# Hybrid decoder step on one core: the down-projections' high and low activation parts side by side, three matmuls under the high weights instead of four

## The reference, cut to what matters

```python
def conv_ffn(h, buf, w_up, conv_w, conv_b, w_down):
    up = h @ w_up
    padded = concatenate([buf, up], axis=1)
    c = conv_b
    for j in range(3):
        c = c + conv_w[j] * padded[:, j:j + l]
    g, v = split(c, 2, axis=-1)
    return (silu(g) * v) @ w_down, padded[:, -2:]
...
x = x + conv_ffn(rmsnorm(x, norm_ffn[i]), ...)
```

## Time and profile before

| | |
|---|---|
| median of 3 runs | 1355.78 us (1355.6, 1355.78, 1358.63) |
| span of the profiled execution, first to last instruction | 1349.1 us |
| the profiled execution's own time | not listed apart from its span |
| TensorE busy | 1239.3 us, 92%, 9702 matmuls |
| weight loads | 1168.9 us, 87%, beside the matmuls |
| VectorE busy | 723.9 us, 54% |
| ScalarE busy | 450.3 us, 33% |
| GpSimd busy | 371.5 us, 28% |
| DMA | 129.12 MB, mean 96 GB/s |

### The profile page before, as it was taken

One profiled execution on the slowest core, in us unless ns is written; L12 is line 12 of the kernel. 1 busy time (PEld: TensorE's weight loads), 2 busy tenths in 40 slices (PEclk: granted clock), 3 DMA queues, 4 the chain that ended last, 5 costly groups with the idle time before them and its releaser, 6 DMA issues.

```text
span 1349.1 us, 25331 instructions
## 1 busy us (share of the span) xinstructions
PE 1239.3 (92%) x9702; PEld 1168.9 (87%) x9710; DVE 723.9 (54%) x1164; ACT 450.3 (33%) x748; POOL 371.5 (28%) x802
## 2 busy tenths in 40 slices
PE   5249869989999999999999799999999999999999
PEld 4249446679999999999998766699999999999998
DVE  5036316756777833777633645045577752477732
ACT  5012224433544412444443112133354431344420
POOL 1003576777777777500002145000000000000000
PEclk9669758999999999999997579599999999999999
DMA  6132121013233432222655313022222232222232
GB/s 203 36 129 83 54 67 40 24 48 116 95 117 109 136 114 99 97 93 93 230 142 138 95 55 108 14 86 88 92 89 87 89 108 95 79 93 93 93 105 97
DMA packets 52918, 129.12 MB, mean 96 GB/s; under 512 B 18124, under 2 KB 21964, under 8 KB 52832
## 3 DMA queue, kind: packets, MB, share of 16 engines
q1 hardware_dynamic: 49920, 117.93, 26.5%
q0 software_dynamic: 2944, 10.49, 2.0%
HBM read 109.89 MB, written 18.21 MB: 95 GB/s over the span
## 4 chain that ended last, share of the span: by engine, by line
PE 82%; DMA 5%; DVE 5%; SPq 4%; ACT 3%; issue 1%; ACTq 0%; DVEq 0%
PE ps L1278 23%; PE ps L1280 23%; PE ps L1279 23%; DMA kc<-in_cache_k 4%; PE ps L1521 4%; SPq L270 3%; PE ps L1517 2%; PE ps L1473 2%; ACT probs L679 2%; DMA w_raw<-in_wqkv 1%; PE ps L1478 1%; DVE probs L1038 1%; PE ps L1369 1%; DVE soft L1022 1%; PE ps L1438 1%
## 5 line engine op out<-in xcount | busy, mean ns | idle before, releaser
L1278 PE MATMUL ps<-hx_hi,w_hi 128*128 128x260 f32 x1600 | 454.1, 284 | 45.4 <-DVE w_lo L829 42.8
L1280 PE MATMUL ps<-hx_hi,w_lo 128*128 128x260 f32 x1600 | 453.2, 283 | 0.0
L1279 PE MATMUL ps<-hx_lo,w_hi 128*128 128x260 f32 x1600 | 451.7, 282 | 0.0
L578 ACT ACTIVATE w_hi<-w_raw 128x1024 fp32r<-128x1024 f32 (+1 forms) x156 | 175.8, 1127 | 548.2 <-PE ps L1280 498.8
L1278 PEld LDWEIGHTS ps<-hx_hi,w_hi 128*128 128x128 f32 x1600 | 302.4, 189 | 46.6 <-issue 43.0
L1279 PEld LDWEIGHTS ps<-hx_lo,w_hi 128*128 128x128 f32 x1600 | 302.2, 189 | 0.1
L1280 PEld LDWEIGHTS ps<-hx_hi,w_lo 128*128 128x128 f32 x1600 | 302.1, 189 | 0.0
L829 DVE TENSOR_TENSOR w_lo<-w_raw,w_hi 128x1024 fp32r<-128x1024 f32 (+1 forms) x156 | 207.7, 1332 | 150.2 <-ACT w_hi L578 150.2
L1278 PE MATMUL ps<-hid_hi,w_hi 128*128 128x260 f32 x704 | 199.1, 283 | 0.0
L1279 PE MATMUL ps<-hid_lo,w_hi 128*128 128x260 f32 x704 | 198.8, 282 | 0.0
L1280 PE MATMUL ps<-hid_hi,w_lo 128*128 128x260 f32 x704 | 198.6, 282 | 0.0
(11 more groups left out here) (224 smaller groups left out, 1776.5 us busy)
## 6 DMA issues: line engine op xcount, KB each, us to landing
w_raw<-in_wup SPq DMA_DIRECT2D x88, 512.0 KB, 3.2
w_raw<-in_wdn SPq DMA_DIRECT2D x32, 704.0 KB, 4.0
w_raw<-in_wglu SPq DMA_DIRECT2D x16, 512.0 KB, 3.2
w_raw<-in_wqkv SPq DMA_DIRECT2D x12, 512.0 KB, 4.4
w_raw<-in_wo SPq DMA_DIRECT2D x8, 512.0 KB, 3.3
g_scr<-rec POOLq DMA_DIRECT2D x8, 512.0 KB, 3.0
c_scr<-rec POOLq DMA_DIRECT2D x8, 512.0 KB, 3.1
wst<-g_scr SPq DMA_DIRECT2D x8, 512.0 KB, 8.1
```

Source lines behind the costliest of these rows:

```text
L578: act.activation(w_hi[b][:, 0:kt * P], w_raw[b][:, 0:kt * P], ACT.Copy).then_inc(hi_done, 1)
L1278: pe.matmul(out, wh, xh, start=(k == 0), stop=False)
L1279: pe.matmul(out, wh, xl, start=False, stop=False)
L1280: ins = pe.matmul(out, wl, xh, start=False, stop=(k == kt - 1))
```

## The change: what it does

The hidden tiles' high and low parts, so far in two arrays, lie in one array `hid_x` with a row of `WX` = 1040 columns for each of the 11 tiles: the high part of the first half (260 columns) followed by 86 columns of its low part, the same for the second half, and then the other 174 low columns of both halves (348 together). `down_unit` replaces `unit` in the four down stages. For each input tile it streams 346, 346 and 348 columns through the high weights and, as before, 260 and 260 through the low weights. High products and the low weights' products accumulate in columns 0 to 260 of the unit's two banks; the low parts' products land in columns 260 to 346 of those banks and in a third bank, 4 + b.

A unit's result is thus in two parts. ScalarE copies the low parts' products to a buffer in SBUF with two activations (172 and 348 columns), after its split of the next weights; VectorE waits for the first copy, adds the main part to `x`, waits for the second copy, adds the buffer to `x`, and then counts `evac`. `hid_hi` is written to two pieces of a row by one instruction, `hid_lo` by two instructions. In dn01 the buffer is `lo_rec`, which lies over `rec`, and ScalarE waits for `scr_out` ahead of the stage; in the other down stages it is `lo_part`. `rec` grows by 16 columns, and its uses name their columns; those lines of the diff are left out below.

```diff
--- before.py
+++ after.py
@@ -31,6 +31,10 @@
+LA = 86
+LC = HALF - LA
+WA, WC = HALF + LA, 2 * LC
+WX = 2 * WA + WC
@@ -96,8 +100,7 @@
-        hid_hi, D0 = place("hid_hi", NPAIR * TOK, F32R)
-        hid_lo, _ = place("hid_lo", NPAIR * TOK, F32R)
+        hid_x, D0 = place("hid_x", NPAIR * WX, F32R)
@@ -123,6 +126,7 @@
+        lo_part = [place(f"lo_part{b}", TOK, at=D1 + 12672 + 2112 * b)[0] for b in range(2)]
@@ -168,7 +172,7 @@
-        rec, REC = place("rec", JQ * 2 * P)
+        rec, REC = place("rec", JQ * 2 * P + 16)
@@ -180,6 +184,7 @@
+        lo_rec = [place(f"lo_rec{b}", TOK, at=REC + 2080 * b)[0] for b in range(2)]
@@ -211,6 +216,22 @@
+        def hid_row(k):
+            return hid_x[:, bass.ds(k * WX, WX)]
+        def hid_hi(k):
+            return hid_row(k)[:, 0:2 * WA].rearrange("p (h n) -> p h n", h=2)[:, :, 0:HALF]
+        def hid_lo_near(k):
+            return hid_row(k)[:, 0:2 * WA].rearrange("p (h n) -> p h n", h=2)[:, :, HALF:WA]
+        def hid_lo_far(k):
+            return hid_row(k)[:, 2 * WA:WX].rearrange("p (h n) -> p h n", h=2)
...
@@ -732,7 +753,7 @@
-                    act.activation(tiles(hid_hi, it), hid[:], ACT.Copy).then_inc(hid_hi_done, 1)
+                    act.activation(hid_hi(it), halves(hid[:]), ACT.Copy).then_inc(hid_hi_done, 1)
@@ -760,7 +781,22 @@
-                stage(f"dn{layer}{half}", residual(2) if (layer, half) == (0, 1) else (lambda it, b, u: None))
+                def down(it, b, u):
+                    act.wait_ge(units_done, u + 3)
+                    act.wait_ge(evac, u + 1)
+                    part = halves((lo_rec if (layer, half) == (0, 1) else lo_part)[b][:])
+                    act.activation(part[:, :, 0:LA], ps[:, 2 * b:2 * b + 2, HALF:WA],
+                                   ACT.Copy).then_inc(sem("near_copied"), 1)
+                    act.activation(part[:, :, LA:HALF], ps[:, 4 + b, 0:WC].rearrange("p (h n) -> p h n", h=2),
+                                   ACT.Copy).then_inc(sem("lo_copied"), 1)
+                    if (layer, half) == (0, 1):
+                        act.wait_ge(evac, u + 3)
+                        norm_in(2, 2 * it + b, b)
+                if (layer, half) == (0, 1):
+                    act.wait_ge(sem("scr_out"), 16 * 3 * NJ)
+                stage(f"dn{layer}{half}", down)
@@ -1103,8 +1139,9 @@
-                    tt(tiles(hid_lo, it), hid[:], tiles(hid_hi, it).bitcast(F32),
-                       ALU.subtract).then_inc(hid_ready, 1)
+                    hi, h2 = hid_hi(it).bitcast(F32), halves(hid[:])
+                    tt(hid_lo_near(it), h2[:, :, 0:LA], hi[:, :, 0:LA], ALU.subtract)
+                    tt(hid_lo_far(it), h2[:, :, LA:HALF], hi[:, :, LA:HALF], ALU.subtract).then_inc(hid_ready, 1)
@@ -1138,7 +1175,23 @@
-                residual(f"dn{layer}{half}", 2 if (layer, half) == (0, 1) else None)
+                def add_down(it, b, u):
+                    m = 2 * it + b
+                    units = 8 * (2 * layer + half) + m
+                    dve.wait_ge(units_done, u + 3)
+                    dve.wait_ge(sem("near_copied"), units + 1)
+                    tt(halves(tiles(x, m)), acc(b), halves(tiles(x, m)), ALU.add).then_inc(sem("hi_added"), 1)
+                    dve.wait_ge(sem("lo_copied"), units + 1)
+                    dve.wait_ge(sem("hi_added"), units + 1)
+                    tt(tiles(x, m), (lo_rec if (layer, half) == (0, 1) else lo_part)[b][:], tiles(x, m), ALU.add).then_inc(evac, 1)
+                def next_norm(it, b, u):
+                    if (layer, half) == (0, 1):
+                        dve.wait_ge(evac, u + 3)
+                        norm_in(2, 2 * it + b, b, isinstance(it, int) and it == 0 and b == 0)
+                stage(f"dn{layer}{half}", add_down, next_norm)
@@ -1279,6 +1332,35 @@
+            def down_unit(stage, n, b, kwait=None):
+                kt = INFO[stage][4]
+                u = BASE[stage] + 2 * n + b
+                pe.wait_ge(lo_done, u + 3)
+                pe.wait_ge(evac, u + 1)
+                for k in range(kt):
+                    if kwait:
+                        pe.wait_ge(kwait[0], kwait[1] + k + 1)
+                    wh, wl = w_hi[b][:, k * P:(k + 1) * P], w_lo[b][:, k * P:(k + 1) * P]
+                    row = hid_x[:, k * WX:(k + 1) * WX]
+                    for h in range(2):
+                        pe.matmul(ps[:, 2 * b + h, 0:WA], wh, row[:, h * WA:(h + 1) * WA],
+                                  start=(k == 0), stop=False, skip_group_check=True)
+                    pe.matmul(ps[:, 4 + b, 0:WC], wh, row[:, 2 * WA:WX],
+                              start=(k == 0), stop=(k == kt - 1), skip_group_check=True)
+                    for h in range(2):
+                        ins = pe.matmul(ps[:, 2 * b + h, 0:HALF], wl, row[:, h * WA:h * WA + HALF],
+                                        start=False, stop=(k == kt - 1), skip_group_check=True)
+                ins.then_inc(units_done, 1)
...
-            stage("dn00", hid_hi, hid_lo, (hid_ready, 0))
+            down_stage("dn00", (hid_ready, 0))
...
-            stage("dn11", hid_hi, hid_lo, (hid_ready, 3 * NPAIR))
+            down_stage("dn11", (hid_ready, 3 * NPAIR))
```

More of the change, by code:

```diff
@@ L459, in tables @@
                 base_step = 0
-                r5 = rec[:].rearrange("p (q r s c) -> p q r s c", q=JQ, r=2, s=CH)
-                r4 = rec[:].rearrange("p (q r n) -> p q r n", q=JQ, r=2)
+                r5 = rec[:, 0:JQ * 2 * P].rearrange("p (q r s c) -> p q r s c", q=JQ, r=2, s=CH)
+                r4 = rec[:, 0:JQ * 2 * P].rearrange("p (q r n) -> p q r n", q=JQ, r=2)
                 def seed(src, s):
@@ L476, in tables @@
                     cmul(j, blk(0, dst, n), blk(1, dst, n), blk(0, src, n), blk(1, src, n), pr, pi, n * GC)
-                pool.dma_start(g_scr[bass.ds(j, 1)].rearrange("o p c -> (o p) c"), rec[:]).then_inc(scr, 16)
+                pool.dma_start(g_scr[bass.ds(j, 1)].rearrange("o p c -> (o p) c"), rec[:, 0:JQ * 2 * P]).then_inc(scr, 16)
                 pool.wait_ge(scr, 48 * j + 16)
@@ L488, in tables @@
                          n * GC, True)
-                pool.dma_start(c_scr[bass.ds(j, 1)].rearrange("o p c -> (o p) c"), rec[:]).then_inc(scr, 16)
+                pool.dma_start(c_scr[bass.ds(j, 1)].rearrange("o p c -> (o p) c"), rec[:, 0:JQ * 2 * P]).then_inc(scr, 16)
                 pool.wait_ge(scr, 48 * j + 32)
@@ L1281, in unit, with down_stage @@
                 ins.then_inc(units_done, 1)
+            def down_unit(stage, n, b, kwait=None):
[17 more added lines that the diff above has]
+                ins.then_inc(units_done, 1)
+            def down_stage(name, ready):
+                down_unit(name, 0, 0, ready)
+                down_unit(name, 0, 1)
+                with pe.Fori(1, INFO[name][3] // 2) as n:
+                    for b in range(2):
+                        down_unit(name, n, b)
             def norm_stat(n):
@@ L1452, in _ @@
             stage("up00", hx_hi, hx_lo, (hx_ready, KT))
-            stage("dn00", hid_hi, hid_lo, (hid_ready, 0))
+            down_stage("dn00", (hid_ready, 0))
             stage("up01", hx_hi, hx_lo, None)
-            stage("dn01", hid_hi, hid_lo, (hid_ready, NPAIR))
+            down_stage("dn01", (hid_ready, NPAIR))
             norm_stat(2)
@@ L1545, in _ @@
             stage("up10", hx_hi, hx_lo, (hx_ready, 2 * KT))
-            stage("dn10", hid_hi, hid_lo, (hid_ready, 2 * NPAIR))
+            down_stage("dn10", (hid_ready, 2 * NPAIR))
             stage("up11", hx_hi, hx_lo, None)
-            stage("dn11", hid_hi, hid_lo, (hid_ready, 3 * NPAIR))
+            down_stage("dn11", (hid_ready, 3 * NPAIR))
 def kernel(**inputs):
```

## The result

Medians: 1364.10 us (16 runs, 1356.96 to 1378.85) against 1356.77 for the kernel before (16 runs beside it, 1334.83 to 1364.34 but for one of 4044.59). The ratio is 1.0159, 95% interval 1.0101 to 1.0217; in a second comparison the medians are 1362.22 and 1354.33, the ratio 1.0121 (1.0071 to 1.0172). The forecast was 1355.8 us, no change, with a range of 1347 to 1360; the kernel is slower than that.

What follows compares the result with a forecast made beforehand. TensorE's own pace in the projections was taken as the bound. Terms -3.5 + 0.6 + 1.1 + 1.6 + 0.2 = 0.0 us gave 1349.1 + 0.0 + 6.7 = 1355.8 us, range 1347.0 to 1360.0.

Steps and rivals of the forecast that it cites:

- The matmul term: Down stages: five matmuls instead of six per row save 10 ns of excess on each of 352 rows, -3.5 us.
- `hid_lo` in two pieces: Four passages from up to down: the tile comes later and TensorE waits 0.1 to 0.2 us each, +0.6 us together.
- The end: End of the program: near copy and second add come between the last matmul and the last store, +1.1 us.
- The end of dn01: Where the norm wants x: copy and two adds delay low weights and sum of squares, so TensorE resumes +1.6 us later.
- The clock: TensorE's longer pause after dn01 could put the norm's four matmuls at the lower clock: +0.2 us, ends -1.7 and +1.7.
- The wait on `scr_out`: On ScalarE ahead of dn01: GpSimd has finished those tables long before, so the wait costs 0.
- the added work inside the stages: Within a stage, ScalarE's copies and VectorE's second add hide behind the units, so no unit waits: 0.
- the columns set the pace: Slower rival, four stages: 0.461 ns a column, rows stay at 719 ns, only added costs remain: +3.5 us, 1359.3; chance 0.18.
- displaced operands: Matmuls of the down stages: operands lying elsewhere could cost 1 ns on five matmuls of 352 rows, 1.8 us lost.
- The 6.7 us from span to median: Added to the profiled span of 1349.1 us to reach the median 1355.78, as work around the span that the change leaves alone.

Runs made afterwards that it cites:

- the paces measured above: Kernel before plus 8 x 64 unread test matmuls behind dn11: float32r with 260, 346, 512 columns took 119.1, 159.2, 233.8 ns start to start.
- the two part kernels: The change in dn00, dn10 and dn11 only, median 1358.44 us, and in dn01 only, 1357.22 us, beside 1354.33 for the kernel before.
- the delayed kernel: Kernel before with 1.8 us more VectorE work ahead of dn01's last sum of squares, lengthening the pause: median 1365.22 us against 1356.78, ratio 1.0032.
- the three stages with the old pause: The change in dn00, dn10 and dn11 only, dn01 as before, pause 3.07 us: median 1358.44 us against 1354.33 for the kernel before, ratio 1.0061.

## Why the prediction was wrong, by its own steps

1. **The matmul term, -3.5 us: the step that failed.** Its measured size is +0.9. A row went from 719.4 to 7.943 us / 11 = 722.0 ns (dn10 and dn11: 63.54 and 63.70 us for 8 units). The split of the excess into a fixed part and a part by the column rested on two single matmuls at the edge of a run: 388 ns for the one that waited for its load, which rightly excluded the load as the bound, and 277 ns for the last one, from which I read 5 ns as the price of the load beside it. The short load shows 1 to 3 ns. The one reading that held over all rows, that the excess vanishes at the lower clock, spoke for the columns and was written under that rival. This term alone is 4.4 us. Most of the +0.9 is in the pace itself: with the paces measured above, six times 119.1 ns against 159.2 + 159.2 + 160.1 + 2 x 119.1, a row gets 2.3 ns longer (160.1 is worked out for 348 columns).
2. **`hid_lo` in two pieces, +0.6.** Too high: TensorE waits 0.34 us for one hidden tile, in dn00, and nowhere else (0.5 us in the other profile of the changed kernel, and nothing in those of the two part kernels). The 0.2 us of the earlier trace rows was the wait of a weight load; its matmuls show no idle time there. dn00 is 0.6 us longer, of which 0.2 are its rows.
3. **The end, +1.1.** Right in its chain, measured +1.2.
4. **The end of dn01, +1.6.** Right: the pause grew by 1.68 us.
5. **The clock, +0.2 with ends of 1.7: the second term that was mis-sized.** The norm's matmuls at the lower level were named (up to 0.9 us) and came (2.10 - 1.14 = 0.96 us). But the whole clock part is 5.7 us on average, and it was not seen. The runs of the kernel before spread from 165 to 255 us at the lower level; 11 of 74 have under 190 and are some 20 us shorter, and of the 27 of the changed kernel none has. The profile of before shows one execution, in which the clock was low behind the norm, and its three times lie within 3 us, so nothing in it showed the other kind. A longer pause costs clock by itself, as the delayed kernel shows; that it is all of the 5.7 us is not shown, since the three stages with the old pause had more time at the lower level too.
6. **The wait on `scr_out` and the added work inside the stages, 0.** Right for the stages: TensorE has no other new wait in them, and they run at 1.00. Not named was the 0.36 us more that it waits for `hx_lo` in up10.
7. **The rival "the columns set the pace"** had the mechanism as far as the runs show it, an excess by the column, and 1359.3 us; with 0.9 for the rows, which it had as displaced operands, that is 1360.2, where the changed kernel stands at equal clock (1360.5). It had a chance of 0.18, and the forecast's range ended at 1360.0.
8. **The 6.7 us from span to median** were put down to the work around the span. In every run listed with both, the time is 1.7 to 2.0 us over its span. The rest was that the profiled execution is shorter than the median one. The two steps 1 and 5 do not hang on it.

Of the 5.2 us, rows (0.9), the end of dn01 (1.7), the end (1.2) and the two waits (0.7) make 4.5. The 0.6 us in the state-space layer may be clock. Open is why the two waits come, and why the clock stays low so much longer in some executions once the stage behind the norm has run at full clock; the profiles show that it does, and not what decides it.

## A version that beats both

The kernel before with its pause filled by matmuls that nobody reads: 1336.4 and 1337.9 us in two sets, 17 and 19 us under the median of the kernel before beside it (ratios 0.9934 and 0.9879), and 24 to 28 under the changed one's medians, measured apart from it. 3 of its 18 runs had over 190 us at the lower level, one of them at 1373.86 us.

## What to carry to other kernels

Before merging matmuls, fit their pace against the number of columns, with the operands' type: only what stands at zero columns can be merged away. And where TensorE waits for a norm between two stages, look at the granted clock of many runs, not of one profile; a longer path there can cost more through the clock than by itself, and idle time filled with spare matmuls was worth five to six times its length here (17 to 19 us for 3.1). Then read the clock of the stages behind as well: here the small matmuls behind the norm, brought to full clock, ended 11 to 17 us sooner, and the kernel lost 8 to 29 us further on in the same layer in four profiles of six.

## What was unexpected of the hardware

- A matmul in float32r costs 0.455 ns a column at full clock and almost nothing beside (119.1, 159.2, 233.8 ns for 260, 346, 512); in bf16 it costs 0.416 ns a column and some 2.5 ns beside (146.8 ns for 346, 215.8 for 512). At the lower clock float32r has 217 ns for 260, no excess.
- A weight load of 32 columns instead of 128 beside a matmul changes the matmul's pace by 1 to 3 ns only, though the load's own record goes from 188 to 108 ns.
- 2.8 us of spare matmuls in one pause took 33 and 48 us of lower clock from the run: the median time at 1.2 GHz was 175 and 171 us in the two sets, against 208 and 219 for the kernel before beside them.
